# One core, two transformer blocks: stores of keys and values issued later, a normaliser's sums taken apart from a scale, softplus and a root kept in PSUM, and the last step finished one half of the tokens at a time

## The reference, cut to what matters

```python
mod = jax.nn.silu(c) @ w_ada[l] + b_ada[l]
shift_m, scale_m, gate_m, shift_f, scale_f, gate_f = jnp.split(mod[:, None, :], 6, axis=-1)
h = rms_norm(x, norm_mix_g[l]) * (1.0 + scale_m) + shift_m
proj = h @ w_in[l]
q, k, v, xs, z, bmat, cmat, dt_raw = jnp.split(proj, split_at, axis=-1)
attn = moba_attention(q, k, v, rel_bias)            # bias rows by distance
dt = jax.nn.softplus(dt_raw + dt_bias)              # in the state model
x = x + gate_m * (concat([attn, ssm]) @ w_out[l])
h = rms_norm(x, norm_ffn_g[l]) * (1.0 + scale_f) + shift_f
...
k = (mem_n @ w_k); v = (mem_n @ w_v)                # memory attention of the second block
...
x = x + swiglu(rmsnorm(x, ln_ffn[l]), ...)
return rmsnorm(x, final_norm)
```

## Time and profile before

| what | us |
|---|---|
| median of three runs | 2735.06 |
| lowest and highest of them | 2727.64, 2739.9 |
| the profiled execution, its whole time | 2729.01 |
| its span in the trace | 2727.2 |
| PE busy | 2659.3 (98%) |
| POOL busy | 2200.6 (81%) |
| ACT busy | 1254.3 (46%) |
| DVE busy | 1159.6 (43%) |

### The profile page before, as it was taken

How to read it: one execution, slowest core, us unless ns; L and a number is a source line. 1 busy time by engine, 2 the same in 40 slices (tenths; PEclk the granted TensorE clock), 3 DMA queues, 4 the chain that set the end, 5 groups by cost and what they waited for, 6 DMA issues and landing times.

```text
span 2727.2 us, 43087 instructions
## 1 busy us (share of the span) xinstructions
PE 2659.3 (98%) x16754; PEld 2393.0 (88%) x16754; DVE 1159.6 (43%) x1331; ACT 1254.3 (46%) x1497; POOL 2200.6 (81%) x889
## 2 busy tenths in 40 slices
PE   8999999998999999999999999999999999999997
PEld 8879898898888888888899988999998888888886
DVE  5676857676465554423354145611211111113223
ACT  5435344545444444444654444533544444444444
POOL 7877766686999999898888755867878888889996
PEclk9999999999999999999999999999999999999999
DMA  9997976674565655455455533534455555555553
GB/s 377 404 413 288 356 293 244 233 253 155 212 255 215 264 215 215 174 195 187 165 191 190 187 137 122 216 140 154 174 191 188 187 186 185 185 185 187 198 187 121
DMA packets 101764, 588.00 MB, mean 216 GB/s; under 512 B 11240, under 2 KB 13416, under 8 KB 45200
## 3 DMA queue, kind: packets, MB, share of 16 engines
q1 hardware_dynamic: 93888, 570.60, 56.0%
q10 hardware_dynamic: 7760, 15.74, 1.7%
HBM read 579.98 MB, written 8.40 MB: 216 GB/s over the span
## 4 chain that ended last, share of the span: by engine, by line
POOL 38%; PE 36%; issue 25%; POOLq 1%; DVE 0%; DMA 0%; ACT 0%; DVEq 0%; SPq 0%; ACTq 0%
POOL w_lo L520 38%; PE ps L1232 11%; PE ps L1234 6%; PE ps L1253 3%; PE ps L1255 3%; PE ps L1257 3%; PE ps L1215 3%; PE ps L1219 3%; PE ps L1217 3%; PE ps L1814 1%; PE ps L1789 1%; POOLq L519 0%; DVE arena L1904 0%; DMA arena<-ada 0%; POOLq L523 0%
## 5 line engine op out<-in xcount | busy, mean ns | idle before, releaser
L520 POOL TENSOR_TENSOR w_lo<-raw,w_hi 128x1024 fp32r<-128x1024 f32 x884 | 2200.2, 2504 | 504.9 <-ACT w_hi L543 502.4
L543 ACT CAST w_hi<-raw 128x1024 fp32r<-128x1024 f32 x884 | 923.8, 1050 | 1149.9 <-PE ps L1234 588.5
L1232 PE MATMUL ps<-a_both,w_hi 128*128 128x512 f32 x3392 | 1192.5, 396 | 12.0 <-DVE a_both L2387 7.4
L1234 PE MATMUL ps<-a_both,w_lo 128*128 128x256 f32 x3392 | 952.5, 281 | 0.0
L1232 PEld LDWEIGHTS ps<-a_both,w_hi 128*128 128x128 f32 x3392 | 637.3, 188 | 165.2 <-issue 9.6
L1215 PE MATMUL ps<-a_both,w_hi 128*128 128x256 f32 x2384 | 687.6, 288 | 13.9 <-POOL w_lo L520 8.1
L1219 PE MATMUL ps<-a_both,w_lo 128*128 128x256 f32 x2384 | 677.0, 284 | 0.0
L1217 PE MATMUL ps<-a_both,w_hi 128*128 128x256 f32 x2384 | 676.9, 284 | 0.0
L1234 PEld LDWEIGHTS ps<-a_both,w_lo 128*128 128x128 f32 x3392 | 642.1, 189 | 0.0
L1215 PEld LDWEIGHTS ps<-a_both,w_hi 128*128 128x128 f32 x2384 | 459.7, 193 | 20.9 <-POOL w_lo L520 9.3
L1217 PEld LDWEIGHTS ps<-a_both,w_hi 128*128 128x128 f32 x2384 | 459.8, 193 | 0.7
(11 more groups left out here) (233 smaller groups left out, 1535.9 us busy)
## 6 DMA issues: line engine op xcount, KB each, us to landing
raw<-stream SPq DMA_DIRECT2D x440, 1024.0 KB, 4.8
arena<-ada SPq DMA_DIRECT2D x185, 512.0 KB, 6.6
work<-ada SPq DMA_DIRECT2D x7, 512.0 KB, 5.6
arena<-memT SPq DMA_DIRECT2D x4, 512.0 KB, 9.6
k_spill<-arena ACTq DMA_DIRECT2D x4, 512.0 KB, 8.4
res<-xT SPq DMA_DIRECT2D x4, 512.0 KB, 11.1
v_spill<-arena ACTq DMA_DIRECT2D x4, 512.0 KB, 7.5
rel_rows<-rel_row ACTq DMA_DIRECT2D x4, 512.0 KB
```

The source lines that it names most:

```text
L520: pool.tensor_tensor(w_lo[:, h % SLOTS], raw_half(h), w_hi[:, h % SLOTS].bitcast(F32), ALU.subtract).then_inc(lo_ready, 1)
L543: act.copy(w_hi[:, base % 4], raw[:, tile_slot, (base % 2) * HALF:(base % 2 + 1) * HALF]).then_inc(hi_ready, 1)
L1232: pe.matmul(o, w_hi[:, h % SLOTS, w], a_both[:, c0 + k], start=first and k == 0, stop=False, skip_group_check=True)
L1234: mm = pe.matmul(o[:, 0, :], w_lo[:, h % SLOTS, w], a_hi[:, c0 + k, :], start=False, stop=last and k == 1, skip_group_check=True)
```

## The change

What it does:

- **Stages and stores.** Eight stages at `arena` 0 to 8191, one for each group, in place of two. The four stores of keys are no longer issued during `xk`; that of values 2 is at its place, values 3 and keys 0 and 1 go after the last `mix_operand`, values 0 and 1 after the second `conv_silu`, keys 2 and 3 after `qkv`+5 and `qkv`+7. The four expansions of the relative rows move from `xs` to `qkv`+9 to +15. ACT waits for stores before it overwrites a stage, SP waits for keys 0 and 1 before rows 82 and 83.
- **Sums and sum.** At n = 40 PE only transposes and runs `ada_sum(0)`; the sums of squares move to n = 43 and the second slice to n = 62. DVE's rows stand at 64 from n = 58 to 62. SP looks two halves further ahead for rows between tiles 12 and 33.
- **`conv_silu` of `bz`** stands four halves later in ACT's list.
- **Softplus**: in 7 of its instructions one operand or the result lies in PSUM; two results are written twice, for readers that need a copy in SBUF, which makes 17 instructions.
- **The feed forward's norm**: logarithm and exponential on ACT in place of root and reciprocal; what DVE refines lies in PSUM.
- **The end**: the last step of `down2` runs all four halves for the first 128 tokens, then for the others; residual, squares, root (10 instructions) and scaling follow for each by itself, and ACT issues two of the stores.

The core of the diff:

```diff
-ROW_POINTS = [(-1, 0), (3, 2), (58, 64), (62, 66), (92, 98), ...
+ROW_POINTS = [(-1, 0), (3, 2), (58, 64), (62, 64), (66, 67), (92, 98), ...
...
         def stage(g):
-            return arena[:, 4096 + g % 2 * 1024:5120 + g % 2 * 1024]
+            return arena[:, g * 1024:(g + 1) * 1024]
...
@@ SP
+                if ADA_AT[n] < 2048 and n < ADA_Z + 4:
+                    sp.wait_ge(spill[ADA_AT[n] // 1024], 16)
...
-                done = rows_by(max(2 * t - 9, -1))
+                done = rows_by(max(2 * t - (7 if 12 <= t < 34 else 9), -1))
...
@@ ACT
-                if h in (10, 18, 26, 34):
-                    spill_out((h - 10) // 8, k_dram[(h - 10) // 8])
...
-                    act.wait_ge(spill[g % 2], 16 * (2 + g // 2))
...
-                    spill_out(4 + g, v_dram[g])
+                    if g == 2:
+                        spill_out(6)
...
-            spill_out(7, v_dram[3])
+            spill_out(7)
+            for g in range(2):
+                spill_out(g)
...
-            for j in range(4):
-                his(hx + 4 + 2 * j, 2)
-                rel_rows(j)
+            his(hx + 4, 8)
...
             conv_silu(G0["xs"] + 1, xs_r[:, 4:8, :], 1)
-            his(hb + 3, 9)
+            for g in range(4, 6):
+                spill_out(g)
+            his(hb + 3, 13)
             conv_silu(G0["bz"], bc_r[:, :, :], 0)
...
+                    if h in (hq + 5, hq + 7):
+                        spill_out(2 + (h - hq - 5) // 2)
...
+                    if h in (hq + 9, hq + 11, hq + 13, hq + 15):
+                        rel_rows((h - hq - 9) // 2)
...
-            act.activation(row_a, ps[:, 4, 0:S], ACT.Sqrt, scale=1.0 / D, bias=small[:, 36:37])
-            act.activation(row_b, ps[:, 4, 0:S], ACT.Identity, scale=1.0 / D, bias=small[:, 36:37])
+            act.activation(row_b, ps[:, 4, 0:S], ACT.Ln, scale=1.0 / D, bias=small[:, 36:37])
+            act.wait_ge(log_ready, 1)
+            act.activation(row_a, row_b, ACT.Exp, scale=-0.5).then_inc(root_ready, 1)
...
@@ PE
                 if n == 40:
                     pe.wait_ge(s_const, 16)
+                    pe.wait_ge(row_ready, 1)
                     pe.wait_ge(fold_ready, 2)
-                    row_sums("mix", (ps[:, 6, 0:S], early4))
-                    pe.wait_ge(row_ready, 1)
                     transposed(row_c, ps[:, 7, S:2 * S])
                     ada_sum(0)
-                if n == 60:
+                if n == 43:
+                    row_sums("mix", (ps[:, 6, 0:S], early4))
+                if n == 62:
                     ada_sum(1)
...
+                def last_step(n):
+                    pe.wait_ge(hl_ready, hs0 + n + 1)
+                    for t in range(2):
+                        for s in range(4):
+                            if t == 0:
+                                wait_half(h)
+                            for k in range(2):
...
@@ DVE, softplus
+            rec, s_ps, p_, dt_ps = [ps[:, 6, 32 * i:32 * i + 32] for i in range(4)]
...
-            link(dve.reciprocal(dts[:, 5, :], dts[:, 4, :]))
+            link(dve.reciprocal(rec, s_ps))
...
@@ DVE, feed forward's norm
-            link(dve.reciprocal(row_a, row_a))
+            u = ps[:, 4, S:2 * S]
+            link(dve.tensor_scalar(u, ps[:, 4, 0:S], 1.0 / D, EPS, ALU.mult, ALU.add))
...
-            link(dve.scalar_tensor_tensor(out=row_b, in0=row_b, scalar=-0.5, in1=row_a, op0=ALU.mult, op1=ALU.mult))
+            link(dve.scalar_tensor_tensor(out=u, in0=u, scalar=-0.5, in1=row_a, op0=ALU.mult, op1=ALU.mult))
...
@@ DVE, end
+            last_out(2, 0)
+            last_out(3, 0)
+            token_root(0)
+            dve.wait_ge(fin_ready, 1)
+            token_scaled(2, 0)
+            last_out(2, 1)
+            last_out(3, 1)
+            token_scaled(3, 0)
+            token_root(1)
+            dve.wait_ge(fin_ready, 2)
+            token_scaled(2, 1)
+            token_scaled(3, 1)
```

More of the change, by code:

```diff
@@ L337, in block_program @@
         bias_landed = [sem("bias_landed0"), sem("bias_landed1")]
-        spill = [sem("spill0"), sem("spill1")]
+        spill = [sem(f"spill{g}") for g in range(8)]
         reload_done, y_scaled = sem("reload_done"), sem("y_scaled")
@@ L716, in _ @@
             his(hx + 12, 1)
+            for g in range(6, 8):
+                act.wait_ge(spill[g], 16)
             conv_silu(G0["xs"], xs_r[:, 0:4, :], 0)
@@ L734, in _ @@
                     his(hb + 19, 8)
[L735 to L736 removed]
+            for g in (0, 1, 4, 5):
+                act.wait_ge(spill[g], 16)
             def qkv_out(g):
@@ L836, in _ @@
             act.wait_ge(sq2_done, k - 1)
-            act.activation(small[:, 37:38], small[:, 36:37], ACT.Sqrt)
+            act.preload_act_table_set("natural_log_exp_and_others")
             for p in range(2):
@@ L1623, in step @@
                                    last and kp == 1)
+                def last_step(n):
+                    pe.wait_ge(hl_ready, hs0 + n + 1)
+                    for t in range(2):
+                        a = slice(t * P, (t + 1) * P)
+                        for s in range(4):
+                            h, c0 = base + 4 * n + s, n % 2 * 4 + 2 * (s % 2)
+                            o = outs_tok[1][s // 2][:, t, :]
+                            if t == 0:
+                                wait_half(h)
+                            for k in range(2):
+                                w = slice(k * 512, k * 512 + 512)
+                                pe.matmul(o, a_hi[:, c0 + k, a], w_hi[:, h % SLOTS, w], start=False, stop=False,
+                                          skip_group_check=True)
+                                pe.matmul(o, a_lo[:, c0 + k, a], w_hi[:, h % SLOTS, w], start=False, stop=False,
+                                          skip_group_check=True)
+                                mm = pe.matmul(o, a_hi[:, c0 + k, a], w_lo[:, h % SLOTS, w], start=False,
+                                               stop=s % 2 == 1 and k == 1, skip_group_check=True)
+                            if s % 2 == 1:
+                                mm.then_inc(tok_done, 1)
                 def first_steps():
@@ L1639, in down @@
                     n0 = 11 * half
+                    apart = half == 1 and name == "down2"
                     if half == 0 and name == "down":
@@ L1647, in down @@
                     step(half, n0, None, True, False)
-                    with pe.Fori(0, 5) as i:
+                    with pe.Fori(0, 4 if apart else 5) as i:
                         step(half, n0 + 1, i, False, False)
                         step(half, n0 + 2, i, False, False)
+                    if apart:
+                        step(half, n0 + 9, None, False, False)
+                        last_step(n0 + 10)
             down("down", 0)
@@ L2164, in _ @@
                     boundary(0)
-                if h == 60:
+                if h == 43:
+                    means("mix", (ps[:, 6, 0:S], D))
+                    root(ps[:, 6, 0:S], ps[:, 6, S:2 * S], row_a)
+                if h == 62:
                     boundary(1)
```

167 lines of the change are left out of this document (91 added, 76 removed).

## The result

| | before | changed |
|---|---|---|
| median of five runs | 2735.06 us | 2718.29 us |
| the profiled execution, its whole time | 2729.01 us | 2716.96 us |
| its span | 2727.2 us | 2714.9 us |

The ratio of the runs is 0.9947, with a 95% interval from 0.9925 to 0.9969. The forecast was 2708 in a range from 2696 to 2722: the time lies inside, 10 us above the forecast. The gain of 16.8 us is 0.6%. The two profiled executions differ by 12.3 us of span, where the sum had said 23.9. The first question is where the other half is.

What follows compares the result with a forecast made beforehand. PE was taken to bound the kernel, busy 98% of the span, so only its stops and half-clock stretches could go. Terms of 23.9 us off 2729.0 gave 2705.1, plus 3 for the runs' level: 2708, range 2696 to 2722.

Steps and rivals of the forecast that it cites:

- the sum: Whole kernel: gains of 5.9, 5.0, 7.3, 0, 1.3 and 4.4 us, together 23.9 us.
- I take 3 of these 6: Runs' median lies 6.0 us above the profiled execution; 3 us of that added to 2705.1, giving 2708.
- n = 40: PE's 3.2 us wait for DVE's squares signal and its half-clock stretch go: 5.9 us gained.
- n = 62: Second slice, from n = 60: 9.4 us of stop and small waits go, 4.4 come back in `xs`; net 5.0, range 3 to 6.
- second rival: At n = 62 row 63's fold comes no sooner, PE stops 6.4 us; 14.1 gained in all, 2718 us; chance 0.08.
- `bz`+12: PE's stop behind ACT's wait for DVE's convolution goes: 8.0 removed, 0.7 lost at `qkv`+4; net 7.3, range 1.9 to 8.0.
- first rival: At `qkv`+4 the rows' loads bound fold 7: 6.1 us of `bz`+12's gain goes, 2714 us; chance 0.20.
- slack about even: At `qkv`+4, PE's slack against fold 7: 1.9 - 8.0 + 8.5 us, softplus freeing rows 8.5 sooner; 0.7 lost.
- Relative rows and keys: Two key stores and four expansions in `qkv`+5 to +15: 9 us of DMA hidden in free time, 0 us; share 0.89.
- slower rival: State model's heads: late ada rows cost 3.3 us a head, 53 us over 16 heads, 2758 us; chance 0.04.
- Norm: Feed forward's norm: first operand sooner, held by an instruction reading SBUF until POOL's end; 1.3 us gained, range 0 to 3.3.
- end: Behind the last product: first 128 tokens finish earlier, last stores issued sooner; about 4.4 us gained, range 3 to 5.5.

Runs made afterwards that it cites:

- `a_n40_old`: The change with the sums of squares back at n = 40 and the second slice back at n = 60, stores as changed; median 2717.12 us.
- `a_silu_old`: The change with the third conv_silu back between `bz`+11 and `bz`+12, its place before; median 2723.58 us.

## Why the prediction was right or wrong

- **The time** lay in the range, 10 us above the forecast. Where in the range it fell was chance: the second five runs of the change have a median of 2706.9, 1 us below the forecast. The step that was off is "I take 3 of these 6": the 6 us between the profile before and the median were taken as a level of the runs. As far as the traces tell, they were mostly one of two distances of PE's pairs in `up`, 8.5 us apart. The profile before, and so the forecast, was on the short side, the profile and the five runs of the result on the long one.
- **n = 40**: 7.3 with a short wait in `xv` (1.2) that went too, without it 6.1 for the 5.9 of the sum. The size was right, by luck, and the reason wrong: the sum credited the move of the squares, and `a_n40_old` shows that the stop goes without it. The signal was late since DVE stood behind late rows; stores and SP's look ahead removed that, in shares that no run tells.
- **n = 62**: 3.9 for 5.0. The fold came 6.0 us sooner (194.4), not 7.7, and PE 1.3 sooner than reckoned (192.7), so 1.8 of the wait stayed. The sum had the stores alone for the fold and nothing for SP's look ahead, which no run parts from them. At the heads the move of sums and slice is worth 0.6 us (`a_n40_old`). The new waits in `xs` were 3.0 without a price of the clock, close to the 3.6. The second rival (fold no sooner) did not happen.
- **`bz`+12**: removed 8.1, as the 8.0 of the sum. The price at `qkv`+4 was 3.9 and not 0.7, and 1.6 were lost at `bz`+8, a late row for which the sum had nothing. Net 2.5 for 7.3; the move of `conv_silu` by itself is worth 5.8, as the 1.6 are lost without it too (`a_silu_old`). This is the first rival, at two thirds of its 6.1, but in one stop with a stretch at 0.50 and not in several. The step that failed is "slack about even". Softplus did shrink by 8.1, but fold 7 came only 13.5 us sooner, where the forecast needed the 5.9 + 5.0 + 8.5 = 19.4 of its own terms, and PE came 17.5 sooner: the rows' places that softplus frees fill DMA (1.02 from 310 to 340 us), and the rows come no faster than that. (17 x 0.2 is 3.4 and not 3.6, as the forecast has it; the 4.0 measured makes that small.)
- **Relative rows and keys**: nothing, as forecast; DMA 0.87 for 0.89. The slower rival did not happen: the one wait of the heads above 2 us is 2.5, as before.
- **Norm** 1.4 for 1.3, **end** 3.7 for 4.4. The Trainium skill, page "Perfetto Trace Analysis", section "Optimizing Scalar/DVE Operations", puts an instruction's fixed cost at about 60 ns on SBUF and 125 ns on PSUM. That difference does not show in this profile either: DVE's four steps took 0.42 to 0.43 us each, three of them with a result in PSUM.
- **The sum** without `up` and the small term behind it: 23.9 forecast, 20.3 measured in the first profile, of which 1.5 behind `qkv`+23 is chance.
- **The signs** that it named: row 63's fold before 194 us (194.4), no wait for it (1.8), and a wait at `qkv`+4 under 1 or about 6 us (2.1, with a stretch at 0.50 behind it) all failed; softplus, the wait at `up` and the end came as said.

## What to carry to other kernels

Compare two profiles at the same products of the engine that bounds, stage by stage, before believing their difference: 8.9 us of this one lay in a stage that the change does not touch, against 12.3 in all. And where a load leaves a queue ahead of a deadline, ask what the next deadline is: of the 4.7 us that the sums and the slice won ahead of `qkv`+4, all but 0.6 was taken back at the next two deadlines, 1.9 at `bz`+8 and 2.3 by fold 7, whose time comes from DVE and DMA in turns. Operands in PSUM are worth it where POOL works on SBUF nearly all the time, until the first instruction that must read SBUF.

## What the runs showed of the hardware

- The pair of products in `up` takes 346.7 or 353.3 ns on average, with PE busy and at the full clock in both. The distance holds for hundreds of microseconds and changes where the pattern is broken: at a wait, at the short products of `ada_sum`, at products put in. Over 1280 pairs it is 8.5 us, 0.3% of this kernel, and it probably is what parts the runs of a kernel into two groups.
- A stop of 1.8 to 2.7 us may be followed by 3.4 us at 0.50 or not, with the same code. At the `ada_sum` ahead of `qkv`+23 PE waits 1.79 us in every profile; the stretch came in 4 of 14. Of the seven profiles with the transposes at their place and a wait of 1.9 to 2.7 there, three had it. Each costs 1.7 us. The wait of 2.5 us for DVE at the end of the heads (L1466) had it in all 14, and the stops of 5.9 us and more behind the first 20 us of the kernel had 6.8 or more. A window of the kernel before and one of the change's second profile, behind that same wait:

```profile
440.80:444.20 3.40, 3.40 (x19) 3.40 (x18) 0.69 (x1) 0.00 (x0) 0.00 (x0) 0.51 0.57 229
```

```profile
423.00:427.00 4.00, 2.21 (x23) 1.91 (x22) 3.85 (x7) 0.71 (x1) 2.35 (x1) 1.00 0.97 400
```

- Small DVE instructions with all operands in SBUF took 1.7 us each beside POOL (9.98 / 6), and 0.23 with one operand in PSUM (1.37 / 6). Taken back to SBUF, softplus cost PE 8.3 us at the heads.
